# A four-layer hybrid decoder step: SSD head products alternating between column groups, own-row selections as transposes

## The reference, cut to what matters

```python
# SSD, per chunk of 128 tokens
cb = jnp.einsum('bclgn,bcsgn->bclsg', cc, bc)
y_diag = jnp.einsum('bclsg,bclsgj,bcsgjp->bclgjp', cb, decay, xdt)
...
y_off = jnp.einsum('bclgn,bcgjpn,bclgj->bclgjp', cc, starts, jnp.exp(acs))
y = (y_diag + y_off)

# HGRN2, per chunk of 16 tokens
qg = qc * jnp.exp(G)
att = jnp.einsum('blhd,bshd->bhls', qg, kc * jnp.exp(-G))
att = jnp.where(causal, att, 0.0)
o = jnp.einsum('bhls,bshv->blhv', att, vc) + jnp.einsum('blhd,bhdv->blhv', qg, S)
```

## Time and profile before

| | |
|---|---|
| median of 3 runs | 2019.58 us (2018.29 to 2019.62) |
| span of the profiled execution | 2015.7 us |
| TensorE busy, share of the span | 97% |
| VectorE, ScalarE, GpSimd | 62%, 46%, 50% |
| mean granted clock of TensorE | 0.986 |
| stages (us from the start) | SSD about 440 to 840, HGRN2 about 1040 to 1440 |

### The profile page before, as it was taken

The page is one execution under the profiler, slowest core; times in us unless marked ns, Lnnn a source line. Parts: engine busy times, 40 slices in busy tenths (PEclk is TensorE's granted clock), DMA queues, the critical chain, the costliest instruction groups (busy, mean ns, idle before and its releaser), DMA issues.

```text
span 2015.7 us, 35615 instructions
## 1 busy us (share of the span) xinstructions
PE 1951.5 (97%) x13890; PEld 1763.9 (88%) x13890; DVE 1244.4 (62%) x2220; ACT 930.6 (46%) x1557; POOL 1008.8 (50%) x1249
## 2 busy tenths in 40 slices
PE   7999999999999999999999999999999999999997
PEld 5998989798888988897889999999998889989976
DVE  5988342426887787755147777777454157874552
ACT  3676522334555555342354444443243347674333
POOL 4776704026555655250356666566631337776602
PEclk8999999999999999999999999999999999999998
DMA  4444476535444544487353444444586344445870
GB/s 130 149 147 135 135 250 231 208 105 174 124 116 132 151 132 140 138 297 241 113 170 108 130 130 130 137 136 146 165 313 211 132 148 141 135 148 166 292 231 27
DMA packets 332615, 324.64 MB, mean 161 GB/s; under 512 B 19768, under 2 KB 313056, under 8 KB 332448
## 3 DMA queue, kind: packets, MB, share of 16 engines
q1 hardware_dynamic: 330944, 321.49, 49.8%
q10 hardware_dynamic: 1504, 0.87, 0.2%
HBM read 292.16 MB, written 29.61 MB: 160 GB/s over the span
## 4 chain that ended last, share of the span: by engine, by line
PE 75%; DVE 14%; ACT 5%; issue 2%; DMA 2%; POOL 1%; SPq 1%; DVEq 0%; ACTq 0%
PE ps L773 10%; PE ps L774 10%; PE ps L778 10%; PE ps L1458 5%; PE ps L1467 4%; PE ps L1261 3%; PE ps L1524 2%; PE ps L888 2%; PE ps L763 2%; PE ps L765 2%; PE ps L764 2%; ACT wh L1713 2%; DVE work L2543 2%; PE ps L1602 1%; PE ps L1541 1%
## 5 line engine op out<-in xcount | busy, mean ns | idle before, releaser
L1693 POOL TENSOR_TENSOR wl<-raw,wh 128x256 fp32r<-128x256 f32 x1216 | 1003.3, 860 | 979.1 <-ACT wh L1713 978.9
L1713 ACT ACTIVATE wh<-raw 128x1024 fp32r<-128x1024 f32 x304 | 311.8, 1053 | 202.1 <-PE ps L778 49.8
L773 PE MATMUL ps<-Hh,wh 128*128 128x320 f32 x1200 | 372.2, 324 | 2.8 <-DVE work L2563 0.9
L774 PE MATMUL ps<-Hl,wh 128*128 128x320 f32 x1200 | 360.4, 314 | 0.0
L773 PEld LDWEIGHTS ps<-Hh,wh 128*128 128x128 f32 x1200 | 230.0, 192 | 11.3 <-DVE work L2427 2.3
L774 PEld LDWEIGHTS ps<-Hl,wh 128*128 128x128 f32 x1200 | 230.4, 192 | 2.1
L2258 DVE TENSOR_SCALAR work<-ps 128x512 f32<-128x512 f32 (+8 forms) x220 | 100.3, 474 | 170.9 <-PE ps L871 39.8
L778 PE MATMUL ps<-Hh,wl 128*128 128x320 f32 x1200 | 201.1, 310 | 0.0
L778 PEld LDWEIGHTS ps<-Hh,wl 128*128 128x128 f32 x1200 | 183.2, 189 | 0.1
L773 PE MATMUL ps<-Oh,wh 128*128 128x320 f32 x512 | 152.2, 310 | 3.7 <-DVE Ol L3004 3.7
L774 PE MATMUL ps<-Ol,wh 128*128 128x320 f32 x512 | 151.1, 308 | 0.0
(11 more groups left out here) (439 smaller groups left out, 3922.0 us busy)
## 6 DMA issues: line engine op xcount, KB each, us to landing
raw<-rg_w_in SPq DMA_DIRECT2D x128, 256.0 KB, 3.5
raw<-hg_w_in SPq DMA_DIRECT2D x128, 256.0 KB, 4.8
raw<-ssd_w_in SPq DMA_DIRECT2D x96, 256.0 KB, 3.9
work<-cache_mem_k SPq DMA_DIRECT2D x40, 512.0 KB, 6.3
work<-cache_mem_v SPq DMA_DIRECT2D x40, 512.0 KB, 5.1
raw<-rg_w_out SPq DMA_DIRECT2D x64, 256.0 KB, 3.6
raw<-x_w_k SPq DMA_DIRECT2D x64, 256.0 KB, 3.6
raw<-x_w_v SPq DMA_DIRECT2D x64, 256.0 KB, 3.7
```

The costliest lines, as they stand in the source:

```text
L773: pe.matmul(ps[:, bank, 0:n], high(half, k), mh[:, k, 0:n], start=(k == 0), stop=False)
L774: pe.matmul(ps[:, bank, 0:n], high(half, k), ml[:, k, 0:n], start=False, stop=False)
L1693: ins = pool.tensor_tensor(out, src, wh[:, parted(n) % HALVES, r:r + 2].bitcast(F32), ALU.subtract)
L1713: act.activation(wh[:, nx.n % HALVES], raw[:, slot, :, half * P:(half + 1) * P], ACT.Copy).then_inc(hi_ready, 1)
```

## The change

In `outputs` the two selections now come first, right behind the waits, the wait for `sd_raw_read` with them. Each is a transpose of `sd_sq` by all 128 columns of the identity in another order: the columns that select the sample's own rows come last, the other 96 ahead of them. The second half is written first, to columns 384 to 511, then the first half to 352 to 479, so that its own 32 columns land at 448 to 479 and what it writes besides falls on columns that L1123's product then fills (320 to 447). The head products behind that alternate: both heads' first chunk, both heads' second chunk, both heads' sample tokens. In `turn_back` each of the four selections is likewise a transpose by 128 columns with the wanted 64 first; what stands behind them is overwritten by the next selection or not read.

```diff
                     bank = 5 + t
+                    pe.wait_ge(*past("sd_raw_read", j + 1))
+                    own_last = ident[:].rearrange("p (g q r) -> p q g r", g=4, q=4)[:, ::-1]
+                    for half in (1, 0):
+                        pe.matmul(ps[:, bank, 352 + 32 * half:480 + 32 * half], sd_sq[:, 2 * half + t, :], own_last, start=True, stop=True, is_transpose=True)
                     pe.matmul(ps[:, bank, 320:448], sd_s1[:, t, :], sd_f[:, 1, P:2 * P], start=True, stop=True)
-                    for n in range(2):
-                        h = 2 * t + n
-                        rows = slice(64 * n, 64 * n + 64)
-                        for T in range(2):
-                            pe.matmul(ps[rows, bank, T * P:(T + 1) * P], sd_xt[:, T, h, :], sd_e[:, T, h, :], start=True, stop=True)
-                        pe.matmul(ps[rows, bank, 256:320], sd_xt[sm, 2, h, :], sd_e[sm, 2, h, 0:64], start=True, stop=True)
-                    pe.wait_ge(*past("sd_raw_read", j + 1))
-                    own = ident[:].rearrange("p (g r) -> p g r", g=4)[:, :, 0:NL]
-                    for half in range(2):
-                        mm = pe.matmul(ps[:, bank, 448 + 32 * half:480 + 32 * half], sd_sq[:, 2 * half + t, :], own, start=True, stop=True)
+                    for T in range(3):
+                        for n in range(2):
+                            h = 2 * t + n
+                            rows = slice(64 * n, 64 * n + 64)
+                            if T < 2:
+                                mm = pe.matmul(ps[rows, bank, T * P:(T + 1) * P], sd_xt[:, T, h, :], sd_e[:, T, h, :], start=True, stop=True)
+                            else:
+                                mm = pe.matmul(ps[rows, bank, 256:320], sd_xt[sm, 2, h, :], sd_e[sm, 2, h, 0:64], start=True, stop=True)
                     mm.then_inc(S(f"sd_y{t}_full"), 1)
...
-                    own = ident[:].rearrange("p (g r) -> p g r", g=4)[:, :, 0:16]
+                    own_first = ident[:].rearrange("p (g q r) -> p q g r", g=4, q=2)
                     for T in range(2):
-                        for low in range(2):
+                        for low in (1, 0):
                             at = T * P + 64 * (1 - low)
-                            pe.matmul(ps[:, 4, at:at + 64], hg_sq[:, T, P * low:P * low + P], own, start=True, stop=True)
+                            pe.matmul(ps[:, 4, at:at + P], hg_sq[:, T, P * low:P * low + P], own_first, start=True, stop=True, is_transpose=True)
```

## The result

The changed kernel takes 2004.0 us (median; 2000.2 to 2006.8), the kernel before 2019.6 us (2012.8 to 2021.0). The ratio is 0.9927 with a 95% interval from 0.9904 to 0.9949, so 15 us less (10 to 19). The forecast was 2008.1 us, 11.5 us less. The time is inside the range; the two stages contributed very differently from the sum.

A forecast was written before the change was run, and what follows sets the result against it. TensorE was taken as the bound (97% busy, 75% of the chain). SSD 9.1 + HGRN2 5.2 - low clock 2.8 = 11.5 us less than 2019.6, so 2008.1 us; 8-in-10 range 1999 to 2015 us.

The forecast's parts named there:

- The arithmetic of the edits: Each SSD `outputs` call 0.84 us (heads) and 0.25 us (selections) shorter, each HGRN2 `turn_back` 0.40 us: 23.8 us of TensorE freed.
- Rival (a): SSD head products: column groups do not overlap, a call saves 0.44 us; 9.5 us less, 2010.1 us, chance 0.11.
- Rival (b): Selections in both stages: permuted identity streams at half speed, 0.22 us a transpose; 5.6 us less, 2014.0 us, chance 0.09.
- passes 1, 2 and 7 save nothing: SSD: TensorE's 2.18 us a pass only lengthen its wait for VectorE's gate read, from 0.9 to 3.1 us; 0 saved.
- the clock's: SSD passes 2 and 7: longer waits bring new low-clock stretches, 2 x 1.4 = 2.8 us lost (bounds 0 and 3.4).
- arrives at the gains (L1144): SSD passes 3 to 6: slack there for VectorE's L2632 lets 1.8 of 2.18 us through each pass, 7.2 us saved.
- The last pass: SSD's last pass: both calls stand back to back with VectorE waiting for them; 1.9 us saved.
- HGRN2: 5.2 us forecast: HGRN2 stage: sixteen `turn_back` calls save 0.40 us each, 6.4 us, of which 5.2 us reach the end.
- the 1.2 us subtracted for waits on weights: HGRN2: in three passes with late weights (L1261 for L1693) the first head's 0.40 us are lost, 6.4 - 1.2.
- rival (d): Slower: transposes count as no work, the clock falls more often in HGRN2 and SSD; 23.8 us lost, 2029.1 us, chance 0.06.
- 6.3 us net: SSD stage in the sum: 9.1 us saved over its passes, less 2.8 us lost to low clock.

The follow-up runs named there:

- hg_twice: Kernel before with HGRN2's selections as transposes, each of the four made twice: 2017.2 us, ratio 1.0001 to the kernel before.
- hg_half: Kernel before with half of the HGRN2 selections left out (second 128 tokens, outputs lack them): 2005.0 us, ratio 0.9942 to the kernel before.
- own_only: Kernel before with SSD's selections alone as transposes ahead of L1123, heads one behind the other: 2015.8 us, ratio 0.9994 to the kernel before.
- ssd_only: Kernel before with the SSD part of the change alone (transposes first, heads alternating): 2015.1 us, ratio 0.9994 to the kernel before.

## Why the prediction was right, and where its steps were wrong

**The arithmetic of the edits was right.** 0.84 and 0.25 us a call (together 1.09, measured 1.12) and 0.40 us a `turn_back` (measured 0.40). Rival (a), no overlap of column groups, is out: the products of the two heads start in pairs. The Trainium skill's rule on weight loads (TensorE: Matmul & The Clock Gate, Part 3) was set against L1114's row; the row decided rightly. The table of measured speedups in the same part of the Trainium skill lists three column tiles at 2.38 times, so the page as a whole did not speak against the overlap; this case's eight products in 0.66 us agree with the table. Rival (b) is out as well: with eight-element runs of the identity the second transpose of an SSD pair starts 0.11 to 0.14 us behind the first, not 0.22.

**That passes 1, 2 and 7 save nothing was right, what it costs was too small.** The waits were forecast at 3.1 us and are 3.5; VectorE's chain from L1074's first half to the end of the gate's read is 0.28 us longer (24.67 and 24.95 us). New stretches of low clock were forecast in passes 2 and 7, at 1.4 us each. They came there, at 571.9 and 800.6 us, but of 6.8 us, and the one that pass 1 already had grew from 3.4 to 6.8 us, which the prediction left out. L1152 (before: L1150) is the first product behind the next projections. Pass 2 is 2.7 us later at L1152 than its late gate read explains (L1114 is 2.59 us later than before, the read's end 2.87, L1152 5.59); in pass 7 the way from L1114 to L1152 is 2.35 us longer, some 0.3 us of it the later read; in pass 1 it is 1.34 us longer, again 0.3 of it the read. The term that failed is the clock's, 2.8 us (bounds 0 and 3.4) where passes 2, 7 and 1 lost 2.7, 2.05 and 1.05 us, together 5.8. By the means it is as large or larger: in three pairs that differ by the SSD part alone the clock falls from 0.9849 to 0.9812, from 0.9887 to 0.9850 (HGRN2 part and whole change) and from 0.9880 to 0.9843 (with the gate's product moved), each time some 7.5 us of full speed; the second pair lies across two batches. Where VectorE's order took the waits away, the clock stayed (0.9877 and 0.9888).

**In passes 3 to 6 the step "arrives at the gains (L1144)" failed.** It looked for the first late reader at the gains and found 1.8 us of slack (1.85 by its own row, in which the read ends at 658.65 and not at 658.70). Between `outputs(j, 1)` and the gains stands the output projection, which waits for `sd_so_ready`, VectorE's copy of the last rows behind the whole convolution; I had not followed that wait. Before, VectorE's copy (L2258) ended at 654.80, about 1.0 us ahead of TensorE's L763; after, L763 waits for it. Pass 4, before and then after:

```profile
654.13 0.67 DVE L2258 TENSOR_SCALAR work<-ps 27x512 f32<-27x512 f32 x1
...
655.84 0.40 PE L763 MATMUL ps<-Oh,wh 128*128 128x320 f32 x1
...
659.47 0.67 DVE L2260 TENSOR_SCALAR work<-ps 27x512 f32<-27x512 f32 x1
...
660.19 0.42 PE L763 MATMUL ps<-Oh,wh 128*128 128x320 f32 x1 [1.17 <-DVE work L2260]
```

Of 2.2 us freed, 1.2 went into that wait, and more into waits for the next readers: 0.6 us for ScalarE's L1965 in passes 3 and 4, 0.2 to 0.3 us for VectorE's L2665 in passes 5 and 6. The passes saved 0.3, 0.3, 0.6 and 0.65 us, 1.9 us for the 7.2 of the sum. The last pass saved 2.15 us, forecast 1.9.

**HGRN2: 5.2 us forecast, 15.8 in the profiled pair, 13 to 14 in the runs of that part alone.** Of the section's 6.4 us some 6 arrive. The waits of the stage hardly changed: those for L1693's product fell from 4.6 to 2.2 us, those for VectorE's L2769 rose by 2.0. Before, then after:

```profile
PE ps L1317 <- DVE work L2769: 0.2, 1, 0.2
...
PE ps L1319 <- DVE work L2771: 2.2, 2, 1.3
PE ps L1263 <- POOL wl L1695: 2.2, 3, 1.8
```

Taken over all fourteen traces, the stage without its waits and without 1.7 us for each stretch of low clock lasts 374.7 to 376.4 us with the long section and 368.8 to 370.5 with the short one, 6 us less; the waits are 0 to 6 us in either group. So the 1.2 us subtracted for waits on weights cannot be found in them. What the sum left out is the clock. In 29 executions of the kernel before its mean is 0.9849, in six with the HGRN2 part 0.9887; (0.9887 - 0.9849) x 2010 us = 7.6 us at full speed, and 6.4 + 7.6 = 14.0 against 13.8 us measured between the means. Over all traces, the five with the long section have 9, 9, 9, 9 and 5 stretches of low clock in HGRN2, the nine with the short one 3 to 8, on average 5.1, against 8.2. The prediction treated the clock there as a risk alone (rival (d)); it went the other way. That the clock is better with a shorter section and not with a denser one is shown by `hg_twice` and `hg_half`. Why a shorter section leaves fewer falls is not shown: it may be where the thin matmuls of `outputs` come to lie in time from head to head. No run shifted the heads without shortening them, so this stays open.

So the total was near by luck: the SSD part was to bring 6.3 us net and brought nothing that can be measured, HGRN2 was to bring 5.2 and brought 13 to 14, and the two errors cancelled. Rival (d) was wrong in its sign for HGRN2, but the clock does decide some microseconds in both stages.

On rival (d)'s mechanism: the Trainium skill (TensorE: Matmul & The Clock Gate, Part 4) says transposes do not count as busy in the same way. `hg_twice` puts eight transposes in the place of eight matmuls, and its mean clock is 0.9844 to the 0.9851 of the kernel before beside it; in HGRN2 no run shows them lowering it. In SSD `own_only` leaves it open, with one new fall and a mean clock of 0.9838 to 0.9849.

## What to carry to other kernels

Where an engine that holds the chain is made faster in a stage that another engine nearly fills, list every wait that it meets behind the edit, in program order, with the slack of each; the first one decides, not the one that looks latest. If the other engine has work that frees a buffer and work that only finishes a result, put the freeing work first: here that alone was worth nothing, the faster TensorE program alone was worth nothing, and both together 14 us. The 3.5 us waits of TensorE cost their own length and, behind them, 1.1 to 2.7 us each at half clock, so such an edit can even lose time, as the heads alone did.

## What the runs showed of the hardware

Products of two heads on the two 64-column halves of the array start 0.01 us apart and run side by side, also when each is an fp32 matmul with two loads. A change from the 128*64 to the 64*64 tile costs 0.09 us: 0.20 us from start to start instead of 0.11. In HGRN2 TensorE was 98% busy by the profile and the granted clock fell all the same. Of the nine falls in the kernel before, seven came behind a run of sixteen matmuls of eight columns each, 0.11 us apart, and two behind waits of 2.1 and 1.8 us; in all fourteen traces 79 of the 87 falls of that stage follow such a run (1.8 to 3.2 us after its start), the other eight a wait of 1.7 to 3.3 us. But each of the sixteen heads has such a run and most are followed by no fall. One fall of either kind in the kernel before, by TensorE's timeline and the windows around it:

```profile
1128.91 1.95 PE L1335 MATMUL ps<-work 128*128 128x8 f32 x16
...
1127.80:1131.40 3.60, 3.60 (x30) 3.41 (x29) 0.94 (x2) 0.00 (x0) 0.00 (x0) 1.00 1.09 345
1131.50:1134.90 3.40, 3.40 (x14) 3.40 (x14) 1.08 (x3) 2.33 (x3) 2.23 (x4) 0.50 1.11 351
...
1281.17 0.35 PE L1261 MATMUL ps<-wh,Hh 128*128 128x256 f32 x1 [2.07 <-POOL wl L1693]
...
1281.70:1285.10 3.40, 3.40 (x18) 3.40 (x17) 1.90 (x3) 0.96 (x2) 3.31 (x4) 0.50 0.45 138
```

Where a wait reached into the low stretch, as in passes 1, 2 and 7 of the changed kernel, the stretch lasted 6.8 us instead of 3.4; with the same waits in `ssd_only` it did so in pass 2 alone. One kernel's executions differ by up to 0.8%, the longer ones mostly at the lower clock: 2008.7 to 2024.9 us over 29 runs of the kernel before, at mean clocks from 0.981 to 0.988.
